# First loads of three stages of a decoder block issued from two queues

## What is computed

```python
h = rmsnorm(x, g_mix); u, q, k, v = split(h @ w_in)            # 512 columns each
y_ssm = s5_mixer(u, a, log_dt, b, c, d_skip, w_glu)            # 32 groups of 16 channels, 64 complex states
y_sb = stick_breaking_attention(rmsnorm(q), rmsnorm(k), v)     # 8 heads of 64, causal
x = x + concat(rmsnorm(y_ssm), rmsnorm(y_sb)) @ w_out
x = x + memory_cross_attention(rmsnorm(x), rmsnorm(mem), w_q, w_kv, w_o)   # 4 heads of 128, 256 memory tokens
x = x + square(relu(rmsnorm(x) @ w_up)) @ w_down
```

## Time and profile before

| | us |
|---|---|
| median of 3 runs | 3163.0 |
| lowest, highest | 3161.86, 3169.12 |
| profiled execution, its own time | 3163.12 |
| its span in the trace | 3161.3 |

### The profile page before, as it was taken

The page is one execution under the profiler, slowest core; times in us unless marked ns, Lnnn a source line. Parts: engine busy times, 40 slices in busy tenths (PEclk is TensorE's granted clock), DMA queues, the critical chain, the costliest instruction groups (busy, mean ns, idle before and its releaser), DMA issues. The chain is left out here.

```text
span 3161.3 us, 42569 instructions
## 1 busy us (share of the span) xinstructions
PE 2914.9 (92%) x15268; PEld 2451.9 (78%) x15268; DVE 1671.4 (53%) x2592; ACT 1349.9 (43%) x2304; POOL 646.1 (20%) x493
## 2 busy tenths in 40 slices
PE   6999976799999977996999689999999999999999
PEld 5888844588989876774788578887888788888887
DVE  5434357577877765544666565557554432244222
ACT  4222225476767753312443355555554422233221
POOL 0101002555555541210000032333332000000000
PEclk9999987999999988998999899999999999999999
DMA  5343345382223114413122334333333533354332
GB/s 168 80 106 75 72 119 72 85 205 54 54 64 83 23 34 113 126 67 153 59 95 69 111 123 134 107 106 103 109 106 119 210 134 120 127 180 173 108 118 95
DMA packets 290895, 336.80 MB, mean 107 GB/s; under 512 B 113808, under 2 KB 187552, under 8 KB 290720
## 3 DMA queue, kind: packets, MB, share of 16 engines
q1 hardware_dynamic: 290736, 334.70, 36.1%
HBM read 240.13 MB, written 93.33 MB: 105 GB/s over the span
## 5 line engine op out<-in xcount | busy, mean ns | idle before, releaser
L2950 DVE TENSOR_TENSOR f_big<-f_h_raw,f_big 128x512 fp32r<-128x512 f32 x256 | 177.0, 692 | 463.2 <-ACT f_big L2789 463.2
L2789 ACT ACTIVATE f_big<-f_h_raw 128x512 fp32r<-128x512 f32 x256 | 161.7, 632 | 497.8 <-PE f_ps_bank L3035 260.0
L2992 PE MATMUL f_ps_bank<-f_big 128*128 128x512 f32 x896 | 353.6, 395 | 20.8 <-DVE f_big L2824 7.4
L2993 PE MATMUL f_ps_bank<-f_big 128*128 128x512 f32 x896 | 351.5, 392 | 0.0
L2994 PE MATMUL f_ps_bank<-f_big 128*128 128x512 f32 x896 | 351.2, 392 | 0.0
L701 POOL TENSOR_TENSOR a_w<-a_on,a_left 128x640 f32<-128x640 f32 (+5 forms) x192 | 282.3, 1470 | 246.0 <-DVE a_left L751 107.4
L841 PE MATMUL a_ps_y<-a_wt,a_v 128*96 128x128 f32 x2176 | 270.1, 273 | 3.6 <-DVE a_yt L774 3.6
L841 PEld LDWEIGHTS a_ps_y<-a_wt,a_v 128*96 128x96 f32 x2176 | 249.0, 164 | 4.3 <-issue 4.3
L751 DVE TENSOR_TENSOR_SCAN a_left<-a_ps_z,a_one 128x896 f32<-128x896 f32 (+7 forms) x128 | 207.3, 1620 | 72.1 <-ACT a_ps_z L713 70.6
L2992 PEld LDWEIGHTS f_ps_bank<-f_big 128*128 128x128 f32 x896 | 170.0, 190 | 59.8 <-issue 16.8
L712 ACT ACTIVATE a_on<-a_ps_z 128x640 f32<-128x640 f32 (+5 forms) x192 | 148.9, 776 | 153.9 <-PE a_ps_z L812 112.1
(11 more groups left out here) (390 smaller groups left out, 6371.1 us busy)
## 6 DMA issues: line engine op xcount, KB each, us to landing
f_h_raw<-a SPq DMA_DIRECT2D x128, 512.0 KB, 3.6
f_w_raw<-in_w_up SPq DMA_DIRECT2D x32, 1024.0 KB, 7.0
a<-f_xr SPq DMA_DIRECT2D x128, 256.0 KB, 3.4
f_w_raw<-in_w_down SPq DMA_DIRECT2D x32, 512.0 KB, 3.7
p_xt<-in_x SPq DMA_DIRECT2D x16, 512.0 KB, 4.5
p_raw<-in_w_in SPq DMA_DIRECT2D x16, 512.0 KB, 5.4
q<-p_raw SPq DMA_DIRECT2D x64, 128.0 KB, 2.6
k<-p_raw SPq DMA_DIRECT2D x64, 128.0 KB, 2.5
```

The costliest lines, as they stand in the source:

```text
L2789: act.activation(a_slot(n, 0), a_raw(m)[:, n % 2, :], ACT.Copy).then_inc(a_high, 1)
L2950: dve.tensor_tensor(a_slot(n, 1), a_raw(n // 2)[:, n % 2, :], a_slot(n, 0).bitcast(F32), ALU.subtract).then_inc(a_low, 1)
L2992: pe.matmul(o, wv(i, 0)[:, k, :], hv(i, 0)[:, k, :], start=(k == 0), stop=False)
L2993: pe.matmul(o, wv(i, 0)[:, k, :], hv(i, 1)[:, k, :], start=False, stop=False)
```

## The change

Three groups of loads are issued by ACT at the head of its stream of the stage, and no longer by SP. Nothing else moves: the same transfers with the same semaphores and waits.

```diff
@@ stick_breaking: load_begin is a function of the stage now, and takes the engine and the heads
+        def load_begin(eng, heads, cols, done_q, done_k):
+            for a in heads:
+                eng.dma_start(q2[a][:, cols].bitcast(F32), q_dram[a, :, cols]).then_inc(done_q, DMA)
+                for dst, part in ((k2_hi[a][0], 0), (k2_lo[a][0], 1)):
+                    for copy in range(2):
+                        eng.dma_start(dst[copy * HEAD:(copy + 1) * HEAD, cols].bitcast(F32),
+                                      k_dram[a, part * HEAD:(part + 1) * HEAD, cols]).then_inc(done_k, DMA)
...
-            load_begin(slice(0, BANK), begin_loaded, begin_loaded)
+            load_begin(sp, range(1), slice(0, BANK), begin_loaded, begin_loaded)
...
-            load_begin(slice(BANK, HALF), q_loaded[0], k_loaded[0])
+            load_begin(sp, range(2), slice(BANK, HALF), q_loaded[0], k_loaded[0])
...
         @block.scalar
         def _(act):
+            load_begin(act, range(1, 2), slice(0, BANK), begin_loaded, begin_loaded)
@@ ssm_scan, taken from SP
-            for h, parts in ((0, (b_re, b_im)), (1, (b_im, b_re))):
-                for x in range(2):
-                    sp.dma_start(b_in[h * PC:(h + 1) * PC, x, :, :], parts[x].rearrange("g p c -> p g c")
-                                 ).then_inc(params_in, DMA)
-            for part_, src in enumerate((c_re, c_im, c_re)):
-                sp.dma_start(c_rows[:, :, part_, :], src.rearrange("(s g) c p -> (g c) s p", s=4)).then_inc(params_in, DMA)
@@ ssm_scan, the same loads ahead of ACT's first wait
+                    act.dma_start(b_in[h * PC:(h + 1) * PC, x, :, :], parts[x].rearrange("g p c -> p g c")
...
+                act.dma_start(c_rows[:, :, part_, :], src.rearrange("(s g) c p -> (g c) s p", s=4)).then_inc(params_in, DMA)
             act.wait_ge(mem_in, MT * DMA)
@@ cross_attention
             load_x(1)
-            for n in range(NP):
-                sp.dma_start(raw(n), w_piece(n)[0]).then_inc(w_loaded[n % RAW], DMA)
             load_x(2)
...
+            for n in range(NP):
+                act.dma_start(raw(n), w_piece(n)[0]).then_inc(w_loaded[n % RAW], DMA)
+
             def split(n):
```

More of the change, by code:

```diff
@@ L1097, in _ @@
         def _(act):
+            for h, parts in ((0, (b_re, b_im)), (1, (b_im, b_re))):
+                for x in range(2):
+                    act.dma_start(b_in[h * PC:(h + 1) * PC, x, :, :], parts[x].rearrange("g p c -> p g c")
+                                 ).then_inc(params_in, DMA)
+            for part_, src in enumerate((c_re, c_im, c_re)):
+                act.dma_start(c_rows[:, :, part_, :], src.rearrange("(s g) c p -> (g c) s p", s=4)).then_inc(params_in, DMA)
             act.wait_ge(mem_in, MT * DMA)
```

## The result

| | before | after |
|---|---|---|
| median of six runs | 3162.65 us | 3180.77 us |
| lowest, highest | 3159.84, 3169.12 | 3179.25, 3184.74 |
| span of the profiled execution | 3161.3 | 3177.5 |

The ratio is 1.0057, with a 95% interval of 1.0045 to 1.0068: the change makes the kernel 18.1 us slower. The forecast was 3165, at most 3174.

What follows compares the result with a forecast made beforehand. PE, busy 2914.9 of 3161.3 us, was taken to bound the kernel, with time to win only in its waits at three heads. +2 - 1.7 + 1.5 = +1.8 us on 3163.1 gave 3165, range 3156.5 to 3174.

Steps and rivals of the forecast that it cites:

- the size of ssm_scan: Head of ssm_scan: +2 us, the middle of the bounds -3.2 and +5.8, rounded up.
- the upper bound of +5.8: ssm_scan: parameters sharing evenly with `w_kv` take 13.2 us for 6.6 us of work, ending at 442 instead of 436.
- The rival's own working: ssm_scan, queues alternating row by row: B waits for `w_kv` rows, parameters end at about 447, 10.8 us later; chance 0.15.
- The 0.8 us of room: ssm_scan: DMA engines, 0.91 then 0.94 busy up to 436, lack only 0.8 us that earlier B issues could fill.
- the rule for that stage: ssm_scan: L1201 moves exactly as much as the end of the seven B and C issues moves from 433.66.
- the size of cross_attention: Head of cross_attention: +1.5 us, the middle of the bounds -0.2 and +3.3.
- The middle of the bounds: cross_attention: +1.5 us taken between -0.2 and +3.3, as nothing showed how two queues share.
- that bound: cross_attention, sharing row by row: 5.8 MB instead of 4.1 MB pass before the fourth weight piece, 3.3 us late.
- the 0.9 us of room in the early stretch: cross_attention: DMA engines 0.76 busy over 6 us early on, some 0.9 us of it usable.
- stick_breaking: Head of stick_breaking: -1.7 us, the DMA engines' room, with bounds -3.0 to 0.
- Issue decides everywhere: Rival, all three heads: each won by the earlier last issue, -6.4 us in sum, 3156.7 us; chance 0.2.
- The change doesn't do what it says: Rival: issuing may be common to both engines, so streams take turns; ssm_scan 0, kernel 3164 us; chance 0.2.
- Large rows go first: Rival: engines alternate between queues row by row, so short B rows wait; +12.4 us, 3175.5 us; chance 0.15.

Runs made afterwards that it cites:

- C first: Kernel before with only B and C issued by ACT, C ahead of B, B on its own semaphore: 3175.3 us against 3164.1.
- the exchanged queues: Kernel before with ACT issuing the eight `w_kv` loads first and SP keeping B and C: 3180.8 us against 3164.8.
- with `w_kv` held: Kernel before with only B and C issued by ACT, and SP issuing `w_kv` after all twelve parameter loads landed: 3164.6 us against 3165.8.

## Why the prediction was wrong, point by point

**Wrong: the size of ssm_scan (+2 forecast, +10.0 measured).** The failed step is the upper bound of +5.8. It let the two queues share the DMA engines' time half and half, and took the middle between that and a gain. What the runs show in its place are turns by rows: while `w_kv` passes, B gets 162 rows per us and not half of its 1670. The prediction had named this, sharing in another way than half, as what would make its size wrong. The end of the seven issues moved by +12.6 us, beyond both bounds. The rival's own working, the parameters through at 447, 10.8 later, was near: the last was in at 448.51. The 0.8 us of room, too, was read from a share that doesn't end at 1 (it was 1.10 from 431 to 433 before, with one queue). The argument that kept the rival's chance at 0.15, that short rows leave the wires idle and two queues could overlap, fell by the windows: 6.2 MB by 448 with either one queue or two.

**Right: the rule for that stage.** L1201 was to move as the end of the seven issues does. Against the stage's start they moved by 12.5, L1201 by 12.6. Both ways that the rule named are late; C first and the exchanged queues show each of them alone. Of the 12.6 the stage gives 2.6 back. 1.6 is the wait of DVE for POOL's tables, which was 8.8 and is 7.2 in the trace after; the rest is within what the stage varies from one execution to the next (from L1201 to its end 179.9 to 184.9 us in the twelve traces).

**Wrong: the size of cross_attention (+1.5 forecast, +7.6 in the trace, +8.1 alone).** Three steps failed. The middle of the bounds was taken, as nothing showed how two queues share; they share by rows, and that bound alone had +3.3. Its list of what runs beside the weights stopped at the fourth x tile, 5.8 MB in all. But SP issues `w_o` as soon as the first weight piece is split (1474.44 in the timeline above), so its queue never runs dry and the weights never run alone. By the fourth piece 6.8 MB have passed in the trace after, at 358 GB/s in the mean of 19.1 us, and 4.1 MB before. And the 0.9 us of room in the early stretch was not won. 2.76 MB more at 402 GB/s are 6.9 us, which is the +6.8 of the first product: 3.3, and 2.6 for the 1.0 MB of `w_o`, and 0.9. No run tells the last two apart. The direction, and `g_row` 1.5 us late (forecast 0.9 to 2.4), were right.

**Right: stick_breaking (-1.7 forecast; -2.2 at the head and -1.5 up to the next stage).** The sign is borne out by the head in three traces (9.2 to 10.0 us against 10.5 to 12.4); the size is within that spread, and the times of the kernel with this part alone don't show it.

**The rivals.** "Issue decides everywhere" is out: with `w_kv` held, the head of `ssm_scan` doesn't gain. "The change doesn't do what it says" is out: the issues of SP and ACT run at the same time at their usual 0.6 us. "Large rows go first" is what happened, +12.4 by its working and +18.1 measured, most of the difference lying in `cross_attention` (7.6 against 3.3). By the rule of the Trainium skill's "DMA: Bandwidth & Descriptors", "Queues, rings and completion order", the time was to be about 3175; the trace agrees in the sign and in the turns, and the measured time lies 6 us above.

**What the range left out** is the rival that came: its 3175.5 lay above the upper end of 3174, and had a chance of 0.15. The high end of `ssm_scan` was from even sharing by time. No row of before showed two queues, and the bound on the slow side should then have been the case in which what is waited for comes last of all that is in flight: 448 for C, and for the weights all that SP can issue until they are in.

## What to carry to other kernels

A single queue is also an order: what is issued first is in first, at the full rate. Before a load gets a queue of its own, list everything that the other queue holds until that load has landed, with its row lengths. If its own rows are the shorter ones and the DMA engines are already busy, expect it late, in the worst case here when all of it was in; with equal rows it got half. Reordering the one queue, with a semaphore of its own for what is needed later, is the change to try instead: here it won 11.0 us. And an engine that computes can be held by its issues, here up to 8.4 us by a single one; what stands behind them on it is then late as well.

## What the runs showed of the hardware

- Two queues on the same 16 DMA engines share by rows: 4 KB rows against 2 KB gave the latter a third (139 of 412 GB/s; 663 rows against 662), 2 KB against 2 KB a half (200 GB/s), and rows of 64 bytes against 2 KB still went about one for one (1455 against 1569).
- Rows of 64 bytes passed at 1670 per us alone, 281 beside rows of 1 KB and 162 beside rows of 2 KB.
- A load of 2048 such rows held its issuer for 7.5 us in the mean (SP) and for 7.7 and 8.4 us (ACT, the fourth of B) beside rows of 2 KB, 4.7 us beside rows of 1 KB, and 2.2 us without `w_kv` on the other queue.
- The DMA share of a window goes well over 1 where two queues are in flight (1.26 at 246 GB/s), and with one queue too where the rows are short (1.10 at 106 GB/s from 431 to 433 before). It is then a sum of overlapping packet times and no longer says how much room is left.
- SP and ACT issued loads at the same time, with no sign that one waited for the other: five each from 632.73 on, at 0.6 us apiece.
